# Two recurrent stages reordered, a third weight buffer for the experts, and modulation tiles and blank rows moved

## The reference, cut to what matters

```
def step(s, inp):                       # delta rule, per chunk, 8 heads, two directions
    v_new = u_i - einsum(w_i, s)
    s_next = s * gl_i + einsum(kd_i, v_new)
    o = einsum(qd_i, s) + einsum(qk_i, v_new)
# u, w come from a unit triangular solve with L = (k beta) k^T * decay, strictly lower

xb = h_pad[buf_tok]                     # tokens sorted by expert
y = (silu(xb @ w1[e]) * (xb @ w3[e])) @ w2[e]      # 32 experts, 2 per token (64 and 8 in layer 2)
```

## Time and profile before

| | |
|---|---|
| median of 3 runs | 4263.6 us (4263.36 to 4266.66) |
| profiled execution | 4264.74 us |
| its span | 4262.4 us |
| mean granted TensorE clock | 0.888 |
| PE busy | 3426.1 us, 80% |
| DVE, ACT, POOL busy | 1298.6, 802.0, 729.2 us |
| DMA | 896.99 MB, mean 210 GB/s |

### The profile page before, as it was taken

How to read it: one execution, slowest core, us unless ns; L and a number is a source line. 1 busy time by engine, 2 the same in 40 slices (tenths; PEclk the granted TensorE clock), 3 DMA queues, 4 the chain that set the end, 5 groups by cost and what they waited for, 6 DMA issues and landing times. The chain is left out here.

```text
span 4262.4 us, 61289 instructions
## 1 busy us (share of the span) xinstructions
PE 3426.1 (80%) x22370; PEld 2092.3 (49%) x22371; DVE 1298.6 (30%) x2473; ACT 802.0 (19%) x1857; POOL 729.2 (17%) x795
## 2 busy tenths in 40 slices
PE   4979898886688885994898866985858779999995
PEld 2458757834344442333454432441535346667662
DVE  2465484523100013114111013017445251111114
ACT  1432242210111111000111112110015112222221
POOL 0014204300211111000211110015200023333323
PEclk7989999987899997996999987988669889999997
DMA  7870011024599996324799985230020229998985
GB/s 262 215 158 1 2 44 28 1 100 186 212 419 411 408 381 241 143 103 169 305 396 419 416 363 217 110 119 0 1 72 1 85 107 365 382 368 321 345 345 197
DMA packets 170520, 896.99 MB, mean 210 GB/s; under 512 B 76376, under 2 KB 79002, under 8 KB 124315
## 3 DMA queue, kind: packets, MB, share of 16 engines
...
## 5 line engine op out<-in xcount | busy, mean ns | idle before, releaser
L1949 PE MATMUL ps<-weight_ring,moe_xT 128*64 128x128 f32 (+1 forms) x2656 | 451.9, 331 | 68.8 <-DMA weight_ring<-in_w_dram 67.9
L1949 PE MATMUL ps<-moe_spare,moe_xT 128*64 128x128 f32 (+1 forms) x2528 | 418.0, 325 | 58.2 <-issue 58.2
L1951 PE MATMUL ps<-weight_ring,moe_xT 128*64 128x128 f32 (+1 forms) x2656 | 452.4, 331 | 0.0
L1949 PEld LDWEIGHTS ps<-weight_ring,moe_xT 128*64 128x64 f32 x2656 | 335.2, 143 | 216.0 <-DMA weight_ring<-in_w_dram 83.7
L1951 PE MATMUL ps<-moe_spare,moe_xT 128*64 128x128 f32 (+1 forms) x2592 | 437.2, 329 | 0.0
L2095 DVE TENSOR_TENSOR moe_act<-moe_sg,ps 64x128 f32<-64x128 f32 (+1 forms) x344 | 118.9, 346 | 1024.4 <-ACT moe_sg L2049 1024.4
L1949 PEld LDWEIGHTS ps<-moe_spare,moe_xT 128*64 128x64 f32 x2528 | 313.0, 140 | 168.2 <-issue 114.0
L1918 POOL COPY moe_xg<-moe_xin 64x1024 f32<-64x1024 f32 x172 | 177.3, 1031 | 1163.8 <-PE ps L1932 869.7
L1951 PEld LDWEIGHTS ps<-weight_ring,moe_xT 128*64 128x64 f32 x2656 | 334.2, 143 | 0.0
L1951 PEld LDWEIGHTS ps<-moe_spare,moe_xT 128*64 128x64 f32 x2592 | 322.3, 141 | 0.0
L2099 DVE COPY moe_y<-ps 128x512 f32<-128x512 f32 x172 | 118.9, 692 | 499.3 <-PE ps L1960 499.1
...
## 6 DMA issues: line engine op xcount, KB each, us to landing
...
expert_rows<-delta_o ACTq DMA_DIRECT2D x1, 25088.0 KB, 132.1
```

Source lines behind the costliest of these rows:

```text
L1949: nc.tensor.matmul(m.ps[0:UR, half, 0:W], xT[:, k, :], gate[:, k, cols], start=(k == 0), stop=(k == KD - 1))
L1951: last = nc.tensor.matmul(m.ps[UR:P, half, 0:W], xT[:, k, :], up[:, k, cols], start=(k == 0), stop=(k == KD - 1))
```

## The change

Seven edits.

1. `delta_scan`: the decay argument and k k^T no longer come from PE. The heads stage copies k k^T to a kept tile (ACT) and sends it to DRAM, and the scan's SP loads it and the cumulated gates (broadcast over partitions) for each step and direction, 24 transfers of 256 KB a scan. The decay arguments, exponentials, expanded inverses and lower matrix of step i+1 are made during step i. DVE copies the new values of both directions first and makes the outputs last. The output's state part uses tile Z, not X.
2. `delta_gates` makes three modulation tiles, not six; `delta_finish` makes five, not two, in two side buffers, and transposes the outputs between the units of z.
3. `blank_rows` is split: 18 units of 256 KB by SP in the first heads stage (98 before, by ACT), 80 by SP in `attention_stage`.
4. In layers 0 and 1 the side set joins ring and spare: three sets take turns.
5. Expert loops of ACT and DVE run the true number of units: `head` (1 to 4), then `more` rounds of 4; five small DVE instructions in dispatch compute both.
6. The gather buffer is zeroed by DVE in four parts.
7. `hgrn_scan`: DVE widens the band of unit u+1 before it waits for the outer products of unit u, and PE and ACT make the output of unit u-2 in place of u-1.

The diff, cut to its core (of DVE's loop in the scan the added and the kept lines):

```diff
-def blank_rows(m, eng, zeros):
-    rows = m.expert_rows[E1 * UR:(UNITS2 + SENDS - 1) * UR, :].rearrange("(u p) d -> p u d", p=UR)
-    eng.dma_start(rows, across(zeros[0:UR, :], UNITS2 + SENDS - 1 - E1)).then_inc(m.rows_blank, 16)
+def blank_rows(m, sp, zeros, u0, u1):
+
...
+            if hg == 0:
+                blank_rows(m, sp, p.o[:, 0, :], E1, UNITS1 + SENDS - 1)
...
+                for t in range(3 * j, 3 * j + 3):
+                    sp.wait_ge(s.kk_moved, t + 1)
+                    sp.dma_start(p.kk_there[t], kk_kept[:, t % 2, :]).then_inc(kk_out[t % 2], 16)
...
-                    pe.wait_ge(s.masked, nt)
+                    pe.wait_ge(s.kk_moved, nt)
...
-            if hg == 0:
-                blank_rows(m, act, p.o[:, 0, :])
...
+                    for t in kk_units.get(u, []):
+                        act.wait_ge(s.kk, t + 1)
+                        if t >= 2:
+                            act.wait_ge(kk_out[t % 2], 16 * (t // 2))
+                            act.wait_ge(s.masked, t - 1)
+                        nc.scalar.activation(kk_kept[:, t % 2, :], kk_bank(t), ACT.Copy).then_inc(s.kk_moved, 1)
...
+        @block.sync
+        def _(sp):
+            gates = p.g_there.rearrange("(x d t h) c -> x d t (h c)", x=2, d=2, h=4)
+            for i in range(steps):
+                for d in range(2):
+                    e, b, t = S2[d], B[d], order[d][i]
+                    if i:
+                        sp.wait_ge(e.lm, LV * i)
+                    sp.dma_start(b["L"], gates[0, d, t].partition_broadcast(P)).then_inc(e.gcb_in, 16)
+                for d in range(2):
+                    e, b, t = S2[d], B[d], order[d][i]
+                    if i:
+                        sp.wait_ge(e.z, LV * i)
+                    sp.dma_start(b["Tm"], p.kk_there[t]).then_inc(e.kk_in, 16)
+
         @block.tensor
         def _(pe):
...
-            def scores(i, d):
-                e, b, t = S2[d], B[d], order[d][i]
-                c = cols(t)
-                if i >= 1:
-                    pe.wait_ge(e.xx, XL * i)
-                for h in range(4):
-                    g = p.g[:, t, 8 * d + 4 * hg + h:8 * d + 4 * hg + h + 1]
-                    if i >= NCT + 1 and h == 0:
-                        pe.wait_ge(e.o_done, lat_count(i))
-                    last = nc.tensor.matmul(hd(bank(d, 2), h), g.to_broadcast([P, P]), p.masks[:, d, :],
-                                            start=True, stop=True)
-                last.then_inc(e.gcb, 1)
-                if i >= 1:
-                    pe.wait_ge(e.vnew, i)
-                for h in range(4):
-                    kt = p.kT[:, h, c:c + P]
-                    last = nc.tensor.matmul(hd(bank(d, 0), h), kt, kt, start=True, stop=True)
-                last.then_inc(e.kk, 1)
-                if t >= NCT:
-                    if i >= NCT + 1:
-                        pe.wait_ge(e.o_s, lat_count(i))
...
+            def turn_inverse(i, d):
                 e, b = S2[d], B[d]
                 pe.wait_ge(e.inv0, i + 1)
-                pe.wait_ge(e.lower, i + 1)
...
             for i in range(steps):
+                for d in range(2):
+                    turn_inverse(i, d)
                 for d in range(2):
                     scores(i, d)
                 for d in range(2):
                     keys_on_state(i, d)
-                for d in range(2):
-                    first_level(i, d)
                 for l in range(LV):
                     for d in range(2):
...
+            for d in range(2):
+                decays(0, d)
+            for i in range(steps):
...
+                if i + 1 < steps:
+                    for d in range(2):
+                        decays(i + 1, d)
...
+            def from_state(i, d):
+                e, b, t = S2[d], B[d], order[d][i]
+                if t >= NCT:
+                    dve.wait_ge(e.q_s, latents(i) + 1)
+                    dve.wait_ge(e.pq, LV * (i + 1))
+                    nc.vector.tensor_tensor(h3(b["Z"]), h3(bank(d, 1)), column(gate(p.egc, t, d), 4, P),
+                                            ALU.mult).then_inc(e.o_s, 1)
...
             for i in range(steps):
+                more = i + 1 < steps
                 for d in range(2):
+                    attention(i, d)
                 for l in range(LV):
                     for d in range(2):
+                        merge(i, l, d)
+                    if l == 0:
+                        for d in range(2):
+                            unseen(i, d)
+                if more:
+                    for d in range(2):
+                        decay_args(i + 1, d)
                 for d in range(2):
+                    new_values(i, d)
+                if more:
+                    for d in range(2):
+                        expand(i + 1, d)
+                for d in range(2):
+                    new_state(i, d)
+                for d in range(2):
+                    from_state(i, d)
+                if more:
+                    for d in range(2):
+                        lower(i + 1, d)
+                for d in range(2):
+                    output(i, d)
...
-    job = ModTiles(m, st, *mod, (2, 3, 6), 1)
+    job = ModTiles(m, st, *mod, (2, 3, 6), 2)
...
-                if u >= 4 and u - 4 < job.n:
-                    job.product(pe, u - 4)
-                if u >= 5 and u - 5 < job.n:
-                    job.spread(pe, u - 5)
-            for t in range(NT):
-                pe.wait_ge(s.ready, t + 1)
-                if t >= 1:
-                    pe.wait_ge(s.evac, t)
-                for k in range(KD):
-                    last = nc.tensor.transpose(m.ps[:, 4 + k // 4, (k % 4) * P:(k % 4 + 1) * P],
-                                               p.o[:, t, k * P:(k + 1) * P], m.ident)
-                last.then_inc(s.turned, 1)
+                if u >= 3:
+                    job.product(pe, u - 3)
+                if u >= 4:
+                    job.spread(pe, u - 4)
+                if u >= 5:
+                    turn(u - 5)
+            job.spread(pe, job.n - 1)
+            turn(NT - 1)
...
+            head, more = ends[:, 0:1], ends[:, 1:2]
+            link(nc.vector.tensor_scalar(more, cur[0:1, E:E + 1], 1.0 / SENDS, 0.5 / SENDS - 0.75, ALU.mult, ALU.add))
+            link(nc.vector.tensor_scalar(more, more, 1.5 * 2 ** 23, None, ALU.add))
+            link(nc.vector.tensor_scalar(more, more, -1.5 * 2 ** 23, None, ALU.add))
+            link(nc.vector.scalar_tensor_tensor(out=head, in0=more, scalar=-float(SENDS), in1=cur[0:1, E:E + 1],
+                                                op0=ALU.mult, op1=ALU.add))
+            link(nc.vector.tensor_copy(r.start[:, E + 2:E + 4], ends[:]))
...
-    bufs = [[ring.slot(first + j) for j in range(3)], [r.spare[:, j, :] for j in range(3)]]
-    lead = 1 if side else 0
-    groups = n_exp // G - lead
-    rounds = groups // 2
-    odd = groups % 2
-    turns = rounds + odd
+    ring_set = ([ring.slot(first + j) for j in range(3)], [ring.loaded[slot[j]] for j in range(3)],
+                [ring.loads(first + j) for j in range(3)])
+    spare_set = ([r.spare[:, j, :] for j in range(3)], m.spare_in, [m.spare_loads + 16] * 3)
+    side_set = (side, m.side_in, [m.side_loads + 16] * 3)
+    sets = [side_set, ring_set, spare_set] if side else [ring_set, spare_set]
+    NS_ = len(sets)
+    groups = n_exp // G
+    rounds, rest = groups // NS_, groups % NS_
...
-            nc.gpsimd.memset(xin[:], 0.0).then_inc(s.zeroed, 1)
-            pool.wait_ge(s.zeroed, 1)
...
+            for b in range(AHEAD):
+                nc.vector.memset(xin[:, b, :], 0.0).then_inc(s.zeroed, 1)
...
+            head, more = head_and_more(dve)
+            with dve.Fori(0, head) as u:
+                unit(u, 0, 32 * u + 32)
+            with dve.Fori(0, more) as v:
                 for b in range(SENDS):
...
+            def spread_out(u):
+                t, h = units[u]
                 if u >= 2:
                     dve.wait_ge(s.a_turned, u - 1)
                 nc.vector.tensor_tensor(dense[:, u % 2, :].rearrange("p (c s) -> p c s", s=SUB),
                                         across(loc[:, h * 4 + t, :], NS), sp_, ALU.mult).then_inc(s.dense, 1)
+
+            spread_out(0)
+            for u, (t, h) in enumerate(units):
+                if u + 1 < len(units):
+                    spread_out(u + 1)
...
-                if u:
-                    output(u - 1)
-            output(len(units) - 1)
+                if u >= 2:
+                    output(u - 2)
+            for u in (len(units) - 2, len(units) - 1):
+                output(u)
...
+            sp.wait_ge(s.blank, 1)
+            blank_rows(m, sp, zeros, UNITS1 + SENDS - 1, UNITS2 + SENDS - 1)
+            sp.wait_ge(m.rows_blank, 32)
...
-        for e in range(1, E1, 2):
+        for e in range(1, E1, 3):
...
-                    modulation(0, 4, 10))
+                    modulation(0, 4, 7))
...
```

(2 more changed lines are left out.)

523 lines of the change are left out of this document (285 added, 238 removed).

## The result

The changed kernel takes 4109.0 us (median of 4 runs, 4104.2 to 4119.2), before 4265.1 in the same series: ratio 0.9632 (95% interval 0.9606 to 0.9657), 156 us less. 4070 was forecast, in a range of 4020 to 4135. Its profiled execution takes 4106.7 us against 4264.7, 158.1 less; the table splits these by stage, each counted from its first instruction to the next stage's (issues of transfers not counted; the last stage to its own last instruction).

What follows compares the result with a forecast made beforehand. Experts of layers 0 and 1 were held bound by weight loads, other touched stages by PE or PE-DVE chains. Terms -12.5 - 13 - 64 - 7 - 49 - 49 = -194.5 took 4264.7 to about 4070, range 4020 to 4135.

Steps and rivals of the forecast that it cites:

- rival A: Scans and recurrence: the clock does not rise; recurrence -12 instead of -49, scans 24 us worse; about 4130; chance 0.18.
- scans: Both scans: fewer PE instructions and reordered DVE work shorten latent steps from 37.6 to 29.4 us; -64 (-20 to -90).
- experts: Expert stages: earlier weight loads, no padded units, split zeroing, less added dispatch work; -49 us (-30 to -60).
- recurrence: Recurrence of layer 2: widening one unit ahead takes units from 7.66 to 4.6 us; -49 (-12 to -60).
- Gates: Gates stage: three modulation tiles instead of six end it earlier; -12.5 us (-11 to -13).
- finish: Finish stage: most of the 20.9 us tail goes, three more modulation tiles cost 11; -7 us (-2 to -10).
- First heads stage: First heads stage: 18 blanking units instead of 98 remove most of the traffic's cost; -13 us (-8 to -15).
- The 80 units in the attention stage: Attention stage: the other blanking takes 107.8 us within 135.1 us of idle DMA; 0 us.
- Rival C: Scans: the new loads come late and stop DVE, then the other engines; +360 us, 4430; chance 0.03.
- Rival B: Everything overlaps: scan steps at PE's 26.4 us, recurrence units at 3.9, expert tails whole; about 4025; chance 0.15.
- The third set: Experts of layers 0 and 1: first weight load starts 12.1 us earlier, so each load-bound chain ends 12.1 earlier; -24.2 us.
- Rival D: Expert stages: the edits give nothing because loads set the rate and the end waits elsewhere; +45 us, 4115; chance 0.02.

Runs made afterwards that it cites:

- experiment 12: Changed kernel with six modulation tiles in gates and two in finish again, transpositions still between the units of z: 4111.0 us, ratio 0.9628.
- experiment 11: Changed kernel with all 98 units of blanking issued by SP in the first heads stage, none in the attention stage: 4149.0 us (one run).
- experiments 7 and 8: Changed scan, DVE making direction 0's outputs before direction 1's new values (7: 4154.5 us), or next step's decay arguments, inverses and lower matrices last (8: 4160.3 us).
- experiment 10: Changed kernel with ACT's and DVE's expert loops rounded up to multiples of four units again: 4117.5 us, ratio 0.9639.
- experiment 2: Changed kernel with hgrn_scan's band of unit u widened at the start of unit u, output still at u-2: 4139.9 us (one run).
- experiments 3 and 4: Changed kernel with the recurrence's output of unit u-1, not u-2, same kernel both times: 4105.0 us (one run), then 4092.5 us, ratio 0.9576.

## Why the prediction was right, and where it was off

The time lies in the range, 39 us above the value, between the forecast and rival A, whose price was 4130. Of the 194.5 us forecast, scans, experts and recurrence fell short by 9, 10 and 21. By its steps:

**Gates**, -12.5 against -12.7, **finish**, -7 against -7.4: right, and experiment 12 shows the price of three tiles in finish (11.8 for 11) and of the interleaved transpositions (17.7 for 18). Where in the stage these lie was forecast less well: the tail behind z's last copy is 9.9 us, not 5, and the stretch ahead of it grew by 3.5, not 11. TensorE spent half clock at the stage's start and in its tail before (means 0.96 and 0.62) and none after (1.00). The two errors cancel in the -7; that part is luck.

**First heads stage**, -13 against -16.3: the size was a little low, since the 24 us that remain disturb nothing. Its sentence "By that rule the move from ACT to SP is worth nothing, and only the smaller size is" is wrong: the queue matters to what is issued behind on it. The rule of the Trainium skill that was cited there ("DMA: Bandwidth & Descriptors", section "Issuing engines are not separate DMA queues"), that another issuing engine gives no bandwidth of its own, holds here: the same 25 MB take 130.1 us from SP and 132.1 from ACT. It does not give the wait of a short transfer, 119.2 us behind them on the same queue and 10.9 on another (experiment 11). The smaller size hid this price: with 98 units on SP the stage is 39 us longer than with 98 on ACT, the new copies included. The 80 units in the attention stage cost nothing, as forecast (134.8 against 135.8).

**Scans**, -64 against -55.0, by the means -57.4. At full clock the mechanism and the sum were right: latent steps at 28.7 (29.4 forecast), -30.7 in the first scan. Both orders were needed for it (experiments 7 and 8). Three terms were off. The first new values come 25.5 us after the stage's start, before 23.7, since the first loads are waited for 8.2 us (0 was forecast, but step 0 has no lead). The tail of outputs gained 0.7 us, not 3 (9.2 to 8.5 from the last new values to the end); the intervals between latent steps made up for it, 8.9 each for 8.2. And rival A came in part: half clock made two steps of the second scan 7 us longer. Rival C did not come: no later load is waited for. Rival B did not either: no latent step is at 26.4.

**Experts**, -49 against -39.5: expert stages -45.6, dispatch +0.9, combine +5.2. The failing step is "The last output still has to land, behind the next stage's prefetch: I take 8, 5.5 and 6.5": experiment 10 shows 6.1, -0.3 and 4.3. In layer 0 the trace itself shows it, 5.4 us behind the last real unit's output for 8. The third set gave 9.8 and 9.1 in its stages for 12.1 each, and a third of that went back in the combine stages behind them: 12 net for 24.2. Its mechanism was right: the first load came 15.7 us nearer to the stage's start, 12.1 and 2.6 of zeroing forecast, and the last real output 13.3 earlier. Rival D, no gain at all, falls.

**Recurrence**, -49 against -28.4, the largest miss. Two errors. The first is arithmetic: "122.6/16 = 7.66 a unit" divided a stretch with the last unit's tail; intervals were 7.39, and there are 15. The second is the step "I take 4.6 a unit for imperfect meeting", right at full clock (4.66 and below), wrong as a mean: eight of the 15 intervals were 4.66 or less, seven 6.3 to 7.3, mean 5.47. With 7.39 and 15 units the forecast's 4.6 would have given 42; the clock took 13 of it. That is rival A in its weaker form: the clock rose, and did not stay.

The forecast held edit 7 to be one thing. It is two: the widening ahead gives all of it (experiment 2), 44 to 47 us by itself, and the outputs two behind take 17 to 20 us away (experiments 3 and 4). So the forecast's -49 was near what its own argument, the widening, brings; the second half of the edit, on which it spent no term, cost the rest. The chain of the unit was read from DVE's and PE's sides only; ACT's copy, which waits for the output to free its buffer, was left out.

The second heads stage is 1.1 shorter, the attention stage 1.0, and all stages that the change does not touch are together 3.3 longer.
